# Decode keys of a sparse-attention step: TensorE transposes replaced by VectorE 32 by 32 turns, with pages loaded in 512-byte pieces

## The reference, cut to what matters

```python
def dsa_sample(q, k, v, qi, ki, wi, cache_k, cache_v, cache_kidx, page_table, layer):
    ...
    scores = indexer_scores(qi, wi, ki_all, qpos, kpos)
    _, sel = lax.top_k(scores, topk)
    ...
    kg = jnp.where(from_past, cache_k[phys, layer, off].astype(jnp.float32), gather(k, n_sel).astype(jnp.float32))
    vg = jnp.where(from_past, cache_v[phys, layer, off].astype(jnp.float32), gather(v, n_sel).astype(jnp.float32))
    return attend_selected(q, kg, vg, valid)
```

## Time and profile before

| | us |
|---|---|
| runs | 752.64, 754.49, 754.61 |
| median | 754.49 |
| the profiled execution | 759.38 |
| its span, first to last instruction | 757.7 |
| TensorE busy | 717.0 (95% of the span) |
| VectorE busy | 464.5 (61%) |
| ScalarE busy | 245.0 (32%) |
| GpSimd busy | 202.2 (27%) |

### The profile page before, as it was taken

The page is one execution under the profiler, slowest core; times in us unless marked ns, Lnnn a source line. Parts: engine busy times, 40 slices in busy tenths (PEclk is TensorE's granted clock), DMA queues, the critical chain, the costliest instruction groups (busy, mean ns, idle before and its releaser), DMA issues.

```text
span 757.7 us, 13976 instructions
## 1 busy us (share of the span) xinstructions
PE 717.0 (95%) x4842; PEld 413.8 (55%) x4842; DVE 464.5 (61%) x976; ACT 245.0 (32%) x559; POOL 202.2 (27%) x329
## 2 busy tenths in 40 slices
PE   4987999999999999999999999999999999879994
PEld 3534444444544555677665556777456677754441
DVE  0204279999999865554556555554747676674435
ACT  3203720114667422222222323222743335430000
POOL 1550005015798722222222222222000002650000
PEclk9989999999999999999999999999999999989998
DMA  9930052042130088898887889886200007400611
GB/s 228 293 109 1 2 204 104 34 146 83 62 113 1 29 266 254 284 351 275 262 277 259 254 255 329 294 270 185 82 1 2 1 2 279 112 15 24 198 42 42
DMA packets 60949, 114.12 MB, mean 151 GB/s; under 512 B 8241, under 2 KB 21634, under 8 KB 60882
## 3 DMA queue, kind: packets, MB, share of 16 engines
q1 hardware_dynamic: 29890, 50.37, 21.1%
q0 software_dynamic: 12512, 40.34, 16.2%
q10 hardware_dynamic: 18480, 22.55, 9.1%
HBM read 106.01 MB, written 7.23 MB: 149 GB/s over the span
## 4 chain that ended last, share of the span: by engine, by line
PE 85%; DVE 3%; DMA 3%; ACT 2%; issue 2%; another core or an unknown queue 2%; ACTq 1%; POOL 1%; SPq 0%; DVEq 0%; POOLq 0%
PE banks L547 16%; PE banks L807 12%; PE banks L793 8%; PE banks L721 7%; PE banks L1072 7%; PE banks L769 4%; PE banks L738 4%; PE banks L895 3%; PE banks L882 3%; PE banks L913 2%; PE banks L685 2%; PE banks L758 2%; PE banks L631 2%; DMA arena<-in_x_prompt 2%
## 5 line engine op out<-in xcount | busy, mean ns | idle before, releaser
L547 PE MATMUL banks<-wbuf,xT 128*128 128x512 f32 (+1 forms) x448 | 150.1, 531 | 3.4 <-issue 3.4
L336 POOL DMA_DIRECT2D arena<-in_cache_v x128 | 68.9, 539 | 198.7 <-issue 198.7
L547 PEld LDWEIGHTS banks<-wbuf,xT 128*128 128x128 f32 (+1 forms) x448 | 66.8, 175 | 80.8 <-issue 74.9
L807 PE MATMUL banks<-wbuf,xT 128*128 128x512 f32 (+1 forms) x288 | 105.0, 530 | 0.0
L1526 DVE TENSOR_REDUCE small<-banks 128x1 f32<-128x512 f32 x32 | 22.1, 691 | 93.0 <-PE banks L738 93.0
L1507 DVE MAX8 small<-arena 64x8 f32<-64x2112 f32 x32 | 75.2, 2348 | 1.3
L1509 DVE MATCH_REPLACE8 arena<-small,arena 64x2112 f32<-64x2112 f32 x32 | 74.7, 2334 | 0.0
L721 PE MATMUL banks<-ident,arena 128*128 128x128 f32 x512 | 68.1, 276 | 0.2 <-DMA arena<-in_cache_k 0.2
L721 PEld LDWEIGHTS banks<-ident,arena 128*128 128x128 f32 x512 | 56.4, 141 | 21.6 <-issue 19.8
L793 PE MATMUL banks<-xT,arena 128*128 128x288 f32 x256 | 67.4, 406 | 0.0
L1270 ACT COPY wbuf<-banks 128x512 f32<-128x512 f32 x64 | 37.2, 582 | 70.0 <-PE banks L721 70.0
(11 more groups left out here) (250 smaller groups left out, 1031.0 us busy)
## 6 DMA issues: line engine op xcount, KB each, us to landing
arena<-in_cache_k SPq DMA_DIRECT2D x128, 256.0 KB, 3.4
arena<-in_cache_v POOLq DMA_DIRECT2D x128, 256.0 KB, 3.9
wbuf<-in_w_in ACTq DMA_DIRECT2D x8, 2048.0 KB, 11.3
arena<-in_w_in ACTq DMA_DIRECT2D x8, 512.0 KB, 6.3
arena<-in_x_prompt SPq DMA_DIRECT2D x4, 512.0 KB, 4.7
wbuf<-in_w_out SPq DMA_DIRECT2D x1, 2048.0 KB, 8.0
xT<-in_w_out SPq DMA_DIRECT2D x1, 2048.0 KB, 13.1
out<-wbuf SPq DMA_DIRECT2D x1, 2048.0 KB, 9.4
```

The lines of the kernel that those rows point to most:

```text
L336: e.dma_start(buf[n % 2][:, i, :], cache[bass.ds(pg, 1), 0].rearrange("a p h d -> p (a h d)")).then_inc(arrived[n % 2], 16)
L547: mm = pe.matmul(psum[a * NS:a * NS + ROWS[t], n % PB, 0:w // split], xT[:, c, t * P:t * P + ROWS[t]], wbuf[:, WB[g], c, a * w // split:(a ...
L807: mm = pe.matmul(psum[a * NS:a * NS + ROWS[t], bank, 0:512 // split], xT[:, c, t * P:t * P + ROWS[t]], wbuf[:, WB[g], c, a * 512 // split: ...
```

## The change

The keys are no longer transposed by TensorE. VectorE's `transpose` turns each 32 by 32 block of a [128, 1024] view in place of block, twice a chunk. For a whole key to come out right, the load has to put each quarter of the 512 floats of a key (a pair of heads, 128 floats, 512 bytes) on its own 32 partitions, 4 keys side by side. A page therefore takes four transfers instead of one, each of 32 partitions by 4 pieces of 512 bytes. The new tokens' queries and keys are brought into the same form by 16 small transfers within SBUF and a VectorE transpose.

The logits of a chunk become 128 rows by 256 keys (64 rows of heads by queries, for each half of the chunk), in eight products of 256 columns in place of four of 512; the maxima and sums of the two halves are joined per sequence by copies across partitions (`across`). Probabilities take 2 transposes a chunk instead of 4, and their copy moves from VectorE to ScalarE; values take 8 products of 256 columns instead of 16 of 128. The decoded outputs of a sequence are turned in the loop (`turn_out`, ScalarE `decoded_out`) and not after it. The zeroing of `qbd` moves to GpSimd, the copies of the prompt's last two query tiles to ScalarE, and the heads' gates are stored in another order, for which the second half of `w_out` is loaded by four transfers instead of one.

```diff
+        def key_pages(e, n):
+            for i in range(4):
+                pg = e.value_load(pages[0:1, 4 * n + i:4 * n + i + 1], min_val=0, max_val=NPAGES - 1)
+                for a in range(4):
+                    e.dma_start(k_buf[n % 2][32 * a:32 * a + 32, i, :].rearrange("c (t f) -> c t f", t=4),
+                                cache_k[bass.ds(pg, 1), 0].rearrange("z (t c) (a h) d -> a c t (z h d)", t=4, a=4)[a]
+                                ).then_inc(k_in[n % 2], 16)
...
                 sp.wait_ge(comb, NSEQ)
-                for n in range(NG):
-                    if n >= 2:
-                        sp.wait_ge(kg_tr, 4 * (n - 1))
-                    page_loads(sp, cache_k, k_buf, k_in, n)
+                key_pages(sp, 0)
+                key_pages(sp, 1)
+                sp.wait_ge(roped, ROPED_Q[NT])
+                for dst, src in ((qst, q_tok), (kst, k_tok)):
+                    for t in range(2):
+                        for a in range(4):
+                            sp.dma_start(dst[32 * a:32 * a + 32, t * P:(t + 1) * P],
+                                         src[32 * t:32 * t + 32, NT, a * P:(a + 1) * P]).then_inc(new_in, 16)
+                for n in range(2, NG):
+                    sp.wait_ge(kg_ok, 2 * (n - 1))
+                    key_pages(sp, n)
...
-                def turn_keys(n, half):
-
-                    if half == 0:
-                        pe.wait_ge(k_in[n % 2], 64 * (n // 2) + 64)
-                    for j in (2 * half, 2 * half + 1):
-                        pe.wait_ge((kg_dve, kg_act)[j % 2], 2 * n + j // 2)
-                        for i in range(4):
-                            mm = pe.transpose(psum[:, KB0 + j % 2, i * P:(i + 1) * P],
-                                              k_buf[n % 2][:, i, j * P:(j + 1) * P], ident[:])
-                        mm.then_inc(kg_tr, 1)
...
                 def logits(n):
...
-                    pe.matmul(bank, pick[:, s * P:(s + 1) * P], bias_s[:, g * 512:(g + 1) * 512], start=True, stop=False,
-                              skip_group_check=True)
-                    for j in range(4):
-                        mm = pe.matmul(bank[32 * j:32 * j + 32, :], queries(s, j), kg[n % 2][:, j, :],
-                                       start=False, stop=(j == 3), skip_group_check=True)
+                    for half in range(2):
+                        pe.matmul(bank[NS * half:NS * half + NS], pick[:, s * NS:(s + 1) * NS],
+                                  bias_s[:, g * 512 + 256 * half:g * 512 + 256 * half + 256], start=True, stop=False,
+                                  skip_group_check=True)
+                    pe.wait_ge(kg_ok, 2 * n + 2)
+                    for e in range(2):
+                        for k in range(4):
+                            half, b = k // 2, 2 * (k % 2) + e
+                            mm = pe.matmul(bank[32 * k:32 * k + 32], qbd_v[:, s, b, :],
+                                           kgv[n % 2][:, 8 * half:8 * half + 8, b, :], start=False, stop=(e == 1),
+                                           skip_group_check=True)
                     mm.then_inc(qk, 1)
...
-                def keys_out(n, j):
-                    dve.wait_ge(kg_tr, 4 * n + j + 1)
-                    if j == 0 and n >= 2:
-                        dve.wait_ge(qk, q_no(n - 2) + 1)
-                    nc.vector.tensor_copy(kg[n % 2][:, j, :], psum[:, KB0, :]).then_inc(kg_dve, 1)
+                def turn_keys(n, half):
+                    if half == 0:
+                        dve.wait_ge(k_in[n % 2], 256 * (n // 2) + 256)
+                        if n >= 2:
+                            dve.wait_ge(qk, q_no(n - 2) + 1)
+                    w = slice(1024 * half, 1024 * half + 1024)
+                    nc.vector.transpose(kg[n % 2][:, w], k_buf[n % 2].rearrange("p g n -> p (g n)")[:, w]).then_inc(kg_ok, 1)
...
                 for n in range(NG + 1):
                     s, g = n // 4, n % 4
                     more = n < NG
-                    apart = g == 1 and s > 0
                     if more:
-                        keys_out(n, 0)
+                        turn_keys(n, 0)
+                        turn_keys(n, 1)
...
-                    if n:
-                        probs_out(n - 1)
...
+                if n >= 6 and n % 4 == 2:
+                    turn_out(n // 4 - 1)
...
+                def across(a, column):
+                    mine, other = column
+                    me.add(nc.vector.tensor_copy(other[0:NS], mine[NS:P]))
+                    me.link(nc.vector.tensor_copy(other[NS:P], mine[0:NS]))
+                    return mine, other
```

More of the change, by code:

```diff
@@ L87, in shape_constants @@
     c["ofseq"] = (np.arange(NS)[:, None] // NNEW == np.arange(NSEQ)[None, :]).astype(np.float32)
+    sel = np.zeros((2, 2, 4, NNEW, 2, 2, 2, NNEW), np.float32)
+    for par in range(2):
+        for a in range(4):
+            for qq in range(NNEW):
+                sel[:, par, a, qq, a // 2, par, a % 2, qq] = 1
+    c["sel"] = sel.reshape(P, NS)
     return c
@@ L281, in hybrid_step @@
         ia, ga = aT[:, :, 0:W2], aT[:, :, W2:D]
-        probs = [carve(512) for _ in range(2)]
-        pT = [carve(512) for _ in range(2)]
-        probs_n, pT_n, acc = carve(P), carve(P), carve(P)
+        probs = [carve(256) for _ in range(2)]
+        pT = [carve(256) for _ in range(2)]
+        probs_n, pT_n, acc = carve(NS)[0:NS], carve(NS)[0:NS], carve(256)
+        osb = [carve(256) for _ in range(2)]
         assert at[0] <= LOADED
@@ L296, in hybrid_step @@
         scaled = [v[:, 18:23] for v in seq]
-        qbd_v = qbd.rearrange("p (s j n) -> p s j n", s=NSEQ, j=4)
+        swap = [v[:, 23:25] for v in seq]
+        qbd_v = qbd.rearrange("p (s b n) -> p s b n", s=NSEQ, b=4)
         spare = wbuf[:, 1].rearrange("p c n -> p (c n)")
-        kg = [spare[:, b * 2048:(b + 1) * 2048].rearrange("p (j n) -> p j n", j=4) for b in range(2)]
+        kg = [spare[:, b * 2048:(b + 1) * 2048] for b in range(2)]
+        kgv = [v.rearrange("p (u b c) -> p u b c", b=4, c=32) for v in kg]
         k_in, v_in = sems("k_in", 2), sems("v_in", 2)
@@ L472, in _ @@
                 sp.dma_start(rope[:], c_rope).then_inc(ki_par_in, 16)
-                for dst, src in ((sameq, c_sameq), (own, c_own), (pick_f, c_pick), (tri, c_tri)):
+                for dst, src in ((sameq, c_sameq), (own, c_own), (pick_f, c_pick), (tri, c_tri), (sel, c_sel)):
                     sp.dma_start(dst[:], src).then_inc(const_in, 16)
@@ L498, in _ @@
                 sp.wait_ge(fill, len(FILLS))
-                for c in range(2):
-                    sp.dma_start(wo[c], wo_rows[:, 4 * c:4 * c + 4]).then_inc(wo_in, 16)
+                sp.dma_start(wo[0], wo_rows[:, 0:4]).then_inc(wo_in, 16)
+                for b in range(2):
+                    for l in range(2):
+                        sp.dma_start(wo[1][DH * l:DH * l + DH, 2 * b:2 * b + 2],
+                                     w_out[0, W2:].rearrange("(b l r d) n -> b l d r n", b=2, l=2, r=2)[b, l]
+                                     ).then_inc(wo_in, 16)
                 sp.wait_ge(ke_ok, len(UPDATES))
@@ L756, in turn_probs @@
                         pe.wait_ge(p_ev, q_no(n - 1) + 1)
-                    for i in range(4):
-                        mm = pe.transpose(psum[:, PTB, i * P:(i + 1) * P], probs[n % 2][:, i * P:(i + 1) * P], ident[:])
+                    for u in range(2):
+                        mm = pe.transpose(turned_probs[:, u * P:(u + 1) * P], probs[n % 2][:, u * P:(u + 1) * P], ident[:])
                     mm.then_inc(p_tr, 1)
@@ L764, in values @@
                     pe.wait_ge(v_in[n % 2], 64 * (n // 2) + 64)
-                    if g == 0 and s:
+                    if g == 0 and s >= 2:
+                        pe.wait_ge(o_ok, s - 1)
+                    if g == 2 and s:
                         pe.wait_ge(o_ok, s)
[L767 to L771, removed]
+                    for u in range(2):
+                        for k in range(4):
+                            half, par = k // 2, k % 2
+                            mm = pe.matmul(group_out(n)[32 * k:32 * k + 32],
+                                           pT[n % 2][:, u * P + 32 * k:u * P + 32 * k + 32],
+                                           by_parity(v_buf[n % 2][:, 2 * half + u, :])[:, par], start=(u == 0), stop=(u == 1),
                                            skip_group_check=True)
@@ L1001, in _ @@
                 turn_gated(NT)
-                for a in range(2):
-                    pe.wait_ge(turned_ev, 2 * (NT + 1) - 1 + a)
-                    for s in range(4):
-                        mm = pe.transpose(psum[:, a, s * P:(s + 1) * P], osb[:, 4 * a + s, :], ident[:])
-                    mm.then_inc(os_tr, 1)
                 def turn_normed(t):
@@ L1262, in _ @@
                 filled((GB_, 0))
-                for t in range(2):
-                    turned_out(act, nc.scalar.copy, tr2_act, ("q", t), SB0 + 1 + t)
```

(10 more changed lines are left out.)

275 lines of the change are left out of this document (154 added, 121 removed).

## The result

| | before | after |
|---|---|---|
| runs, us | 747.29, 752.64, 754.49, 754.61 | 816.56, 820.29, 825.06, 825.95 |
| median | 753.57 | 822.67 |
| profiled execution | 759.38 | 816.56 |
| span | 757.7 | 814.9 |

The changed kernel is slower: ratio 1.093, 95% interval 1.083 to 1.102. Medians are of all executions; the ratios and their intervals leave out the two that ran in the chip's slower state (851.90 and 782.93, in the last two experiments). The forecast was 792 in a range of 762 to 835, so the side and the range held; the growth, 69 us by the medians and 57.2 by the two profiled executions, was larger than the 37 forecast. The profiled execution is the fastest of the four after, and the one before is slower than all four beside it in the table; that is why the two differences differ.

The account below looks back on a forecast made before the run. TensorE and SP's queue were taken to pace the kernel before, SP's issuing the changed loop. At 10.0 us a step the loop ends 36.5 us later, all else zero: 796 profiled, 4.9 less for the median, said as 792, range 762 to 835.

Parts of the forecast that it names:

- What bounds the loop: Decode loop: SP's issuing of 4 page numbers and 16 transfers sets the step, 10.0 us; all others wait for it.
- the clock: TensorE in the loop: idling 4 us of every 10 lowers its mean clock to 0.6 to 0.9; SP's pace hides it.
- The time saved on TensorE: Decode loop: fewer transposes save 2.5 of 8.5 us a step, 80 us were TensorE the bound; worth nothing under SP's pace.
- 1.2 us a turn: VectorE's key transposes in the loop: 1.2 us each, 2.4 a step; VectorE comes to 5.3 us and does not set the pace.
- the step of 10.0 us: SP's issuing in the loop: four pages of 2.5 us each make a step; the ends are 8.4 and 11.8.
- I take 0.45: a page 1.15 + 3 x 0.45 = 2.5: SP's key loads: a page's first transfer costs 1.15 us, each of the other three 0.45.
- the upper end: SP's second to fourth transfers of a page: at most 0.6 us each, 0.45 plus some 0.15 of register work and queue waiting.
- what followed its last issue: Loop's end: after SP's last issue the chunk lands, is turned and its logits end, 7.1 us in all.
- Rival 1: Key loads: writing 32 partitions halves the DMA rate, keys take 6.8 us, a step 10.7, time 813; chance 0.2.
- Rival 2: SP's second to fourth transfers: at the bare 333 ns a step is 8.4 us, the loop ends 11.7 sooner, 743; chance 0.09.
- Rival 3: TensorE in the loop: at half clock it becomes the bound, 12 us a step, 112 us more, 866; chance 0.05.
- Rival 4: Key loads: landing slower than 7.6 us makes SP wait for buffers; at 10 a step is 11.2, time 828; chance 0.06.

Follow-up runs that it names:

- the last two experiments: Kernel before with each key page in four loads: 841.35 us, ratio 1.110; changed kernel with SP and ScalarE queues, quarters ordered 0, 2, 1, 3: 774.92 us, ratio 1.018.
- two-queue kernels: Changed kernel, from chunk 2 SP issuing pages 0 and 1, ScalarE's queue pages 2 and 3: 782.31 us; the same with loads writing all 128 partitions: 743.65 us.

## Why the prediction was right or wrong

**What bounds the loop: right.** It named SP's queue, which no busy share shows. SP waits once, before the loop; VectorE waits for key loads; the clock (mean 0.83 from 300 to 560 us, 0.6 to 0.9 forecast) is as written. TensorE is busy for 196 of 260 us, 7 and 8 tenths where 6 or 7 were forecast. Cutting the loads to a quarter gives 710, putting them alone on the old kernel gives 841.

**The time saved on TensorE: worth nothing while SP paces the loop, as forecast; its size was wrong.** The prediction has TensorE at 6.0 us a step, 2.5 saved and 80 us in all. The kernel with one load a page has it at 6.8: 1.7 saved and 54 us, and it gained 53. The prediction added up durations, but one group starts before the other has drained: by starts, eight key transposes held TensorE for 0.87 us (373.94 to 374.81) and not for 1.04. The `turn_out` of each sequence came into the loop besides, and was not in the sum. The time of the changed kernel doesn't depend on this, since SP's pace hides it. That TensorE's "6 us then take 8 or so" came out (196.04 / 260 x 10.72 = 8.1) is luck: it does more work than forecast, at a better clock.

**VectorE: right.** 1.2 us a turn forecast, 1.22 measured; all its other work fits.

**The size: too small by 20.7 us in the profiled executions (57.2 for 36.5), by one term, the step of 10.0 us.** Issuing 30 chunks took 325.9 us and not 300, for three reasons.

- "I take 0.45: a page 1.15 + 3 x 0.45 = 2.5": the loads start 0.50 apart and a page takes 2.57, so a step is 10.28; over 30 steps 8 us. It is so little by luck: the three loads behind the first cost 17 us more than forecast, and the first, 1.07 us and not 1.15, some 10 less. The 0.45 was drawn from issues with fixed addresses, and constant addresses indeed give 0.47; I did not add the register work to the value I took, only to the upper end.
- The larger part was missing altogether: single issues that take up to 1.5 us instead of 0.32. Of 480 in the loop 43 took over 0.35, together 13 us beyond the usual, 0.4 a step. The rows that I read had such issues (L336's maximum is 975 ns beside a median of 333, L1233's 7437 beside 375), and I used medians only. Still they would have told a part: of the 120 key loads in the loop before, 3 were over 0.35, 1.0 us together, which for 480 is 4 us.
- Some 5 us more are lengthened gaps between issues (326 less 308 less 13).

Against the 26 stand 5: SP began 4.8 us earlier than forecast (256.9 for 261.7), and what followed its last issue took 6.7 for 7.1. That start isn't of the change: when this kernel was run again, VectorE's first turn came at 260.2, not at 253.8. So it is luck that the profiled execution shows a miss of 21 us; by the medians it is 31 (822.67 for 792).

**Rival 1, the DMA engines: real, but second.** It put the cost of 32 partitions at a halved rate, 6.8 us for a chunk's keys and a step of 10.7. The two-queue kernels show it with SP out of the way: 9.3 us with 32 partitions, 8.0 with 128; of these the keys take 5.0 and 3.8, three tenths more, and the values 3.7 and 3.1. Without the halved rate its sum holds: 3.8 for keys in 512-byte pieces, 3.2 for values and 0.75 for weights, 7.8 in all, against the 7.56 of the kernel with one load a page in such pieces.

**Rival 2, cheaper issuing: wrong**, though the bare issue did take 0.32 us: the starts are 0.50 apart, and 0.47 without register work. (Its sum is slightly off: at 8.4 us a step the loop ends 11.5 us sooner, not 11.7.) **Rival 3, the clock: wrong as forecast.** TensorE is at half the clock in parts of the loop and not behind every idle: of the 32 chunks' logits 14 took 1.07 us, 12 took 1.93 or 1.94 and 6 lay between. The idle pays for it. **Rival 4, landing:** the median is 3.5 us and the longest 10.2; SP never waited for a buffer inside the loop.

**Open:** what makes single issues slow. They are there with all partitions (10.9 us beyond the usual in the loop) and on the old kernel (13.6) as with 32 partitions (13.2, and 15.1 when run again), and there is more of it with constant addresses and no register work (24.8). In the changed kernel the 36 slowest began with 5.9 key loads under way on average, all others with 4.7, and the DMA engines were busy for 0.94 of the microsecond before them, for 0.82 before the others. That would fit a queue that fills up behind loads still running; no run tests it.

## What to carry to other kernels

Before a load is cut into parts, count what its queue issues in a step: here 4 page numbers and 4 loads took 4.4 us of a step of 8.5, and 16 loads 10.3, whatever they moved. Price an issue from issues that stand back to back, with the register work that they will have; add what the issues beyond the median sum to, and not the median alone; and look at what SP waits for now, since that wait is all the room there is. Price a saving on an engine by the distance between starts: durations of pipelined work overlap, and summed they gave 80 us here where TensorE gave up 54. Such a saving is worth only the distance to the next limit: with one load a page it was worth 53 us, in 512-byte pieces 35 (763.1 less 728.39), and behind SP's sixteen loads nothing.

## What the runs showed of the hardware that was not expected

Back to back loads of 64 KB over all partitions from SP start 0.47 us apart at constant addresses with an issue of 0.43, and 0.51 apart with register work and an issue of 0.33; loads of 32 partitions start 0.50 apart with an issue of 0.32. Loads that write 32 partitions at a time moved 261 GB/s together with the values and weights where loads over all 128, in the same pieces and number, moved 294; with one load a page it was 316 in 512-byte pieces and 343 in 2 KB rows.
